# Building a relative-bias table on TensorE from masks made on GpSimd, in place of 305 VectorE steps

## The reference

```python
NUM_BUCKETS, MAX_DISTANCE = 32, 128
def t5_bucket(rel):
    n = jnp.maximum(rel, 0)
    max_exact = NUM_BUCKETS // 2
    log_ratio = jnp.log(jnp.maximum(n, 1).astype(jnp.float32) / max_exact) / math.log(MAX_DISTANCE / max_exact)
    large = max_exact + (log_ratio * (NUM_BUCKETS - max_exact)).astype(jnp.int32)
    large = jnp.minimum(large, NUM_BUCKETS - 1)
    return jnp.where(n < max_exact, n, large)
# in each block of 128 queries, for the selected keys:
bias = rel_bias[t5_bucket(q_pos[:, :, None] - k_pos)]          # rel_bias: 32 buckets x 8 heads
logits = jnp.einsum('bqhd,bqkhd->bqkh', q, k_sel) * a_scale + bias

def conformer_conv_mixer(h, w_in, conv_w, conv_b, ln_g, ln_b, w_out):
    val, glu_gate, z = jnp.split(h @ w_in, 3, axis=-1)
    u = causal_depthwise_conv(val * jax.nn.sigmoid(glu_gate), conv_w) + conv_b    # 31 taps, 2048 channels
    u = jax.nn.silu(layer_norm(u, ln_g, ln_b))
    return (u * jax.nn.silu(z)) @ w_out
```

## Time and profile before

| | us |
|---|---|
| median of three runs | 2084.09 |
| lowest, highest | 2082.16, 2085.47 |
| the profiled execution | 2082.0 |
| its span in the profile | 2080.2 |
| PE, DVE, ACT, POOL busy | 1895.7, 1620.2, 1079.7, 301.1 |
| mean granted PE clock | 0.962 |

### The profile page before, as it was taken

How to read it: one execution, slowest core, us unless ns; L and a number is a source line. 1 busy time by engine, 2 the same in 40 slices (tenths; PEclk the granted TensorE clock), 3 DMA queues, 4 the chain that set the end, 5 groups by cost and what they waited for, 6 DMA issues and landing times.

```text
span 2080.2 us, 32564 instructions
## 1 busy us (share of the span) xinstructions
PE 1895.7 (91%) x12370; PEld 1702.1 (82%) x12370; DVE 1620.2 (78%) x3041; ACT 1079.7 (52%) x1928; POOL 301.1 (14%) x380
## 2 busy tenths in 40 slices
PE   7897999989999999989979988988887987889997
PEld 6897888868889899889968876877886986779996
DVE  6988788978889998599976866778888576686666
ACT  6887644423354444478855444444445444454554
POOL 3876000000000000087800000020001000010000
PEclk9998999989999999999989999999999999999998
DMA  6344455634446776344535632537775352344652
GB/s 219 124 162 132 162 183 186 229 111 142 132 139 219 236 236 204 112 139 145 171 111 162 206 110 82 183 121 268 273 266 181 122 151 78 103 161 153 206 189 71
DMA packets 93756, 342.29 MB, mean 165 GB/s; under 512 B 10400, under 2 KB 10528, under 8 KB 92960
## 3 DMA queue, kind: packets, MB, share of 16 engines
q1 hardware_dynamic: 93600, 340.20, 49.9%
HBM read 339.11 MB, written 1.05 MB: 164 GB/s over the span
## 4 chain that ended last, share of the span: by engine, by line
PE 56%; DVE 30%; ACT 11%; issue 2%; DMA 0%; POOL 0%; SPq 0%; DVEq 0%; ACTq 0%
PE ps L98 55%; DVE wl L114 9%; ACT tmp L104 6%; DVE ps L124 5%; DVE tmp L124 3%; ACT wh L107 3%; DVE B L124 2%; DVE XS L114 2%; DVE tmp L114 1%; DVE B L114 1%; DVE tmp L119 1%; DVE raw L124 1%; ACT B L104 1%; DVE sm L136 1%; PE ps L101 1%
## 5 line engine op out<-in xcount | busy, mean ns | idle before, releaser
L98 PE MATMUL ps<-XS,wh 128*128 128x256 f32 (+1 forms) x5072 | 955.2, 290 | 39.9 <-DVE wl L114 27.4
L98 PEld LDWEIGHTS ps<-XS,wh 128*128 128x128 f32 (+1 forms) x5072 | 807.9, 195 | 65.4 <-issue 40.6
L114 DVE TENSOR_TENSOR wl<-raw,wh 128x1024 fp32r<-128x1024 f32 (+1 forms) x493 | 591.8, 1228 | 180.5 <-ACT wh L107 180.5
L98 PE MATMUL ps<-XS,wl 128*128 128x256 f32 (+1 forms) x2536 | 726.6, 287 | 0.0
L107 ACT CAST wh<-raw 128x1024 fp32r<-128x1024 f32 (+1 forms) x493 | 496.0, 1038 | 98.6 <-PE ps L98 92.8
L98 PEld LDWEIGHTS ps<-XS,wl 128*128 128x128 f32 (+1 forms) x2536 | 495.4, 195 | 0.0
L114 POOL TENSOR_TENSOR B<-B,tmp 128x236 f32<-128x236 f32 (+10 forms) x352 | 268.3, 800 | 775.1 <-ACT tmp L104 775.1
L98 PE MATMUL ps<-wh,os 128*128 128x512 f32 x864 | 291.0, 405 | 27.8 <-DVE os L114 18.9
L124 DVE SCALAR_TENSOR_TENSOR ps<-B,C,ps 128x254 f32<-128x254 f32 (+17 forms) x576 | 224.5, 469 | 8.3 <-ACT ps L104 8.3
L98 PEld LDWEIGHTS ps<-wh,os 128*128 128x128 f32 x864 | 167.9, 194 | 67.0 <-DVE os L114 20.8
L98 PE MATMUL ps<-wl,os 128*128 128x512 f32 x432 | 173.4, 401 | 0.0
(11 more groups left out here) (155 smaller groups left out, 1950.2 us busy)
## 6 DMA issues: line engine op xcount, KB each, us to landing
raw<-in_w SPq DMA_DIRECT2D x623, 512.0 KB, 4.4
raw<-in_w SPq DMA_DIRECT2D x12, 384.0 KB, 3.9
B<-in_ln SPq DMA_DIRECT2D x4, 1024.0 KB, 6.8
C<-in_cst SPq DMA_DIRECT2D x1, 1309.5 KB, 8.2
X<-in_x SPq DMA_DIRECT2D x2, 512.0 KB, 4.6
out_x<-X SPq DMA_DIRECT2D x4, 256.0 KB, 2.5
cb<-in_cb SPq DMA_DIRECT2D x1, 512.0 KB, 13.2
raw<-in_w SPq DMA_DIRECT2D x2, 256.0 KB, 3.3
```

Source lines behind the costliest of these rows:

```text
L98: return NOTHING if self.e is None else self.e.matmul(*a, **k)
L114: return NOTHING if self.e is None else self.e.tensor_tensor(o, a, b, op)
```

## The change

The table is computed as steps. A bias of bucket b is the sum over all buckets up to b of (bias of the bucket minus bias of the one before). For one key there are 32 comparisons "distance at least the start of bucket k", so four keys fill 128 rows of a mask. POOL makes such a mask (128 rows by 128 queries) with one `tensor_scalar` on the positions; PE multiplies it with a block-diagonal of the bias steps (128 x 32, `rblk`, four keys by eight heads) and gets the bias of 128 queries, four keys and eight heads. 96 masks make the table. Sixteen fill a PSUM bank, which ACT copies into `Bz` (`act_bias`). Masks lie in a ring of eight half buffers (`rep`).

The work stands in a0 and a1. POOL makes 16 masks at the start, then eight ahead of its additions for pair p (p = 0 to 3 in a0, 0 to 5 in a1). PE multiplies 16 ahead of everything, then eight at the end of iteration p (p = 1 to 4 in a0, 1 to 6 in a1). All calls of `bias` on DVE are gone. In stage c, the places that had no ada piece of layer 0 left now take 12 of layer 1, so that f0 has 28 in place of 40. The position row, now with 64 columns of key positions, and a first part of the constants are loaded ahead of X.

```diff
+NPOS = T + 64
+RING = 8
+BURSTS = (4, 6)
+
 CONSTS = (
-    [(f"a_norm{j}", 8) for j in range(2)]
+    [("bstart", 1), ("rblk", 32), ("rblk0", 32)]
+    + [(f"a_norm{j}", 8) for j in range(2)]
...
             if kind == "z" and i >= 2:
                 out.append((f"c.o{i - 1}", [("c_w_out", 0, 128 * (i - 1), 128, 0, D)], "split"))
             n_pair += 1
-            for _ in range(1):
-                a = next(u, None)
-                if a is not None:
-                    out.append(ada_piece(0, a))
+            a = next(u, None)
+            if a is not None:
+                out.append(ada_piece(0, a))
+            else:
+                out.append(ada_piece(1, next(u1)))
...
     b, u = plan_b()
-    out = plan_a(0) + b + plan_c(u) + plan_a(1)
-    u = iter(range(48))
+    u1 = iter(range(48))
+    out = plan_a(0) + b + plan_c(u, u1) + plan_a(1)
+    u = u1
     for l in range(2):
         out += plan_m(l, u) + plan_f(l, u)
...
         cst, posr, cbr, xin, out, lnr = self.ios
+        sp.dma_start(self.m["pos"][:], posr).then_inc(s["pos"].sem, 16)
+        sp.dma_start(self.m["C"][:, 0:NFIRST], cst[:, 0:NFIRST]).then_inc(s["const0"].sem, 16)
         for tb in range(2):
             sp.dma_start(self.X[:, tb, :], xin[:, tb, :]).then_inc(s[f"x{tb}"].sem, 16)
-        sp.dma_start(self.m["C"][:], cst).then_inc(s["const"].sem, 16)
-        sp.dma_start(self.m["pos"][:], posr).then_inc(s["pos"].sem, 16)
+        sp.dma_start(self.m["C"][:, NFIRST:NCONST], cst[:, NFIRST:NCONST]).then_inc(s["const"].sem, 16)
         for i in range(NRAW):
             self.load(sp, i)
         sp.dma_start(self.m["cb"][:], cbr).then_inc(s["cb"].sem, 16)
...
         if j == 0:
+            self.pe_bias(pe, 16, 7)
             pe.wait_ge(*s["const"][0])
         self.pe_entry(pe, A, self.xnt)
         bank, prior = self.a_order()
...
                 stats(2 * p - 3)
                 if p < 8:
                     pair("z", p - 2)
+            if 1 <= p <= BURSTS[j]:
+                self.pe_bias(pe, 8, 3)
         stats(14)
         stats(15)
         pe.wait_ge(*s["norm"][(A, "m"), "root"])
...
         if j == 0:
             self.act_rms(act, A, lambda tb, h: s[f"x{tb}"][0], "a_norm0", True)
+            self.act_bias(act, 0, 7)
             act.wait_ge(*s["cb"][0])
             act.wait_ge(*s["const"][0])
             act.activation(self.m["cb"][:], self.m["cb"][:], ACT.Silu).then_inc(s["lut"].up("silu"), 1)
...
         for p in range(9):
             at = 12 if p - 1 >= 2 else 0
+            if p % 2 and 3 <= p <= BURSTS[j] + 1:
+                self.act_bias(act, 2 * j + (p - 1) // 2, 3)
             if p < 8:
                 for n, (kind, m) in enumerate((("g", 0), ("g", 1), ("v", 0), ("v", 1))):
                     self.feed_act(act, f"{A}.{kind}{p}.{m}")
...
         n = 0
+        if j == 0:
+            self.pool_bias_begin(pool)
+            self.pool_masks(pool, 16)
+        else:
+            pool.wait_ge(*s["norm"][A, "root"])
         for p in range(8):
+            if p < BURSTS[j]:
+                self.pool_masks(pool, 8)
             before = {2 * p: None, 2 * p + 1: None}
...
-        return b[:, 0:3072].rearrange("p (h s) -> p h s", h=8), b[:, 3072:3456], b[:, 3456:3840]
-
-    def bias_step(self, dve, n):
...
-    def bias(self, dve, n):
+        return b[:, 0:3072].rearrange("p (h s) -> p h s", h=8), b[:, 3072:3072 + NPOS]
+
+    def mask(self, n):
+        i = n % RING
+        return self.m["rep"][i // 2][:, (i % 2) * 128:(i % 2) * 128 + 128]
+
+    def pool_bias_begin(self, pool):
+        s = self.s
+        Bz, pf = self.bias_views()
+        pool.wait_ge(*s["pos"][0])
+        pool.tensor_copy(pf, self.m["pos"][:]).then_inc(s["bias"].up("pf"), 1)
+        pool.wait_ge(*s["const0"][0])
+        pool.tt(self.c("rblk", 0, 32), self.c("rblk", 0, 32), self.c("rblk0", 0, 32), ALU.subtract).then_inc(
+            s["bias"].up("steps"), 1)
+        pool.wait_ge(*s["bias"]["pf"])
+
+    def pool_masks(self, pool, n):
+
+        s = self.s
+        Bz, pf = self.bias_views()
         for _ in range(n):
-            if self.nbias < 17 + 32 * 9:
-                self.bias_step(dve, self.nbias)
-                self.nbias += 1
+            x = self.nmask
+            self.nmask += 1
+            q, g = (0, x) if x < 32 else (128, x - 32)
+            if x >= RING:
+                pool.wait_ge(*s["table"][x - RING])
+            pool.ts(self.mask(x), pf[:, q:q + 128], pf[:, T + g:T + g + 1], self.c("bstart"), ALU.subtract,
+                    ALU.is_ge).then_inc(s["mask"].up(x), 1)
+
+    def pe_bias(self, pe, n, bank):
+
+        s = self.s
+        pe.wait_ge(*s["bias"]["steps"])
+        for _ in range(n):
+            x = self.nbias
+            self.nbias += 1
+            pe.wait_ge(*s["mask"][x])
+            if x and x % 16 == 0:
+                pe.wait_ge(*s["evac"]["bias", x // 16 - 1])
+            a = 32 * (x % 16)
+            pe.matmul(self.ps[bank][:, a:a + 32], self.mask(x), self.c("rblk", 0, 32), start=True, stop=True).then_inc(
+                s["table"].up(x), 1)
+
+    def act_bias(self, act, e, bank):
+        s = self.s
+        Bz, pf = self.bias_views()
+        k0 = 64 * e if e < 2 else 128 + 64 * (e - 2)
+        act.wait_ge(*s["table"][16 * e + 15])
+        act.activation(Bz[:, :, k0:k0 + 64], self.ps[bank].rearrange("p (k h) -> p h k", h=8), ACT.Identity).then_inc(
+            s["evac"].up(("bias", e)), 1)
 
 
 
...
                 if n >= 8:
-                    dve.wait_ge(*s["bias"]["add", 31, 7])
+                    dve.wait_ge(*s["evac"]["bias", 5])
...
         put(f"q_norm{l}", vec(inp["q_norm_g_2"][l]))
         put(f"kv_norm{l}", vec(inp["kv_norm_g_2"][l]))
-    put("rel_bias", np.broadcast_to(np.asarray(inp["rel_bias_2"]).reshape(1, 256), (128, 256)))
+    rel = np.asarray(inp["rel_bias_2"], np.float32)
+    steps = np.zeros((2, 4, 32, 4, 8), np.float32)
+    for k in range(4):
+        steps[0, k, :, k, :] = rel
+        steps[1, k, 1:, k, :] = rel[:-1]
+    put("rblk", steps[0].reshape(128, 32))
+    put("rblk0", steps[1].reshape(128, 32))
...
     pos = np.asarray(arrays["positions_2"], np.int32).reshape(T)
-    posr = np.empty((128, T + 2), np.int32)
+    posr = np.empty((128, NPOS), np.int32)
     posr[:, 0:T] = pos[None, :]
-    posr[:, T:T + 2] = pos.reshape(2, 128).T
```

More of the change, by code:

```diff
@@ L45 @@
 _at = 0
+NFIRST = 65
 for _name, _n in CONSTS:
@@ L151 @@
 SIGNALS = [
-    "const", "x0", "x1", "pos", "cb", "out",
+    "const", "const0", "x0", "x1", "pos", "cb", "out",
     "cast",
@@ L180 @@
     "bias",
+    "mask",
+    "table",
     "select",
@@ L240, in plan_b, with plan_c @@
     return out, u
-def plan_c(u):
+def plan_c(u, u1):
     out = []
@@ L373, in __init__ @@
         self.lows = self.casts = 0
-        self.nbias = 0
+        self.nbias = self.nmask = 0
         self.adas = {}
@@ L1071, in bias_views @@
         b = self.m["B"][2]
-        return b[:, 0:3072].rearrange("p (h s) -> p h s", h=8), b[:, 3072:3456], b[:, 3456:3840]
-    def bias_step(self, dve, n):
-        s, m = self.s, self.m
-        Bz, dist, bk = self.bias_views()
-        eq = [m["sc"][:], dist]
-        up = s["bias"]
-        if n == 0:
-            pf = self.tmp[5][:, 0:T + 2]
-            dve.tensor_copy(pf, m["pos"][:]).then_inc(up.up("pf"), 1)
-            dve.wait_ge(*up["pf"])
-            for o, k, w in ((0, 0, 128), (128, 1, 256)):
-                dve.ts(dist[:, o:o + w], pf[:, 0:w], pf[:, T + k:T + k + 1], -1.0, ALU.subtract,
-                       ALU.mult).then_inc(up.up(("n", k)), 1)
-            dve.wait_ge(*up["n", 1])
-            dve.ts(dist, dist, 0.0, None, ALU.max, None).then_inc(up.up("n"), 1)
-            dve.wait_ge(*up["n"])
-            dve.ts(bk, dist, 15.0, None, ALU.min, None).then_inc(up.up(("bk", 0)), 1)
-        elif n <= 16:
-            dve.wait_ge(*up["bk", n - 1])
-            dve.stt(bk, dist, float(bucket_starts()[n - 1]), bk, ALU.is_ge, ALU.add).then_inc(up.up(("bk", n)), 1)
-        else:
-            b, h = (n - 17) // 9, (n - 17) % 9 - 1
-            if h < 0:
-                dve.wait_ge(*up["bk", 16])
-                if b >= 2:
-                    dve.wait_ge(*up["add", b - 2, 7])
-                dve.ts(eq[b % 2], bk, float(b), None, ALU.is_equal, None).then_inc(up.up(("mask", b)), 1)
-            else:
-                r = self.c("rel_bias", b * 8 + h)
-                dve.wait_ge(*up["mask", b])
-                if b == 0:
-                    dve.ts(Bz[:, h, :], eq[0], r, None, ALU.mult, None).then_inc(up.up(("add", b, h)), 1)
-                else:
-                    dve.wait_ge(*up["add", b - 1, h])
-                    dve.stt(Bz[:, h, :], eq[b % 2], r, Bz[:, h, :], ALU.mult, ALU.add).then_inc(
-                        up.up(("add", b, h)), 1)
@@ L1364, in values @@
                 dve.tensor_copy(ct, self.ps[2][:, 0:32]).then_inc(s["soft"].up(("b", "ct")), 1)
-            self.bias(dve, 6)
         for n in range(3):
@@ L1372, in dve_b @@
```

(10 more changed lines are left out.)

5 lines of the change are left out of this document (3 added, 2 removed).

## The result

| | before | after |
|---|---|---|
| median, us | 2083.12 (2077.64 to 2085.47) | 2131.34 (2125.48 to 2135.06) |
| ratio | | 1.0233, 95% interval 1.0199 to 1.0266 |
| profiled execution | 2082.0 | 2125.48 |
| its span | 2080.2 | 2123.7 |

The forecast was 2087, with a range of 2070 to 2101: the sign was right, the size was not.

What follows compares the result with a forecast made beforehand. It took four engines in step to bound a0's convolution and DVE the first pairs of stage c. Terms +28 - 10.8 - 9.3 - 5 = +2.9 on the 2084.1 median gave 2087 us, range 2070 to 2101.

Steps and rivals of the forecast that it cites:

- I take 0.3, a burst of 2.4, between 1.9 and 3.4: Stage a: a POOL mask takes 0.3 us, so a burst of eight takes 2.4, ends 1.9 and 3.4.
- the large term: Stage a, added work: 11 us lost in a0 and 17 in a1, together 28, ends 17 and 38.
- A burst of 2.4 us would fit into POOL's idle 3.42 ahead of a pair.: Stage a: a mask burst fits POOL's idle time by length; only the order, waiting for PE, doesn't fit.
- There z ends 8 and then 11 us late: a1, pairs 4 and 5: fourth multiplications become 13.5 and 16.6 us late, plus 0.6 for a copy: 17 lost.
- The bytes ahead of the last constant stay nearly the same ... I take 0.: Start: DVE's first instruction stays near 9.9 us, 16 masks fit ahead; 0 change, ends 1 gained and 2 lost.
- Stage c: DVE loses 137 table steps and gains 12 adaptation pieces; PE's waits go: 10.8 us gained, ends 8 and 12.
- Stage b: Table steps leave places where PE was fed late: 5 us gained, ends 3 and 13.
- f0: Twelve adaptation pieces leave its last six half pairs, 8.44 us each in place of 10.03: 9.3 gained, ends 7 and 10.
- POOL's wait stays on POOL: Rival, stage a: ACT and PE have more room, only POOL's lack shows; loss 17 for 28, 2076 us; chance 0.26.
- The clock stays up in the attention's entry: Rival, 428.9 to 446 us: 2.4 GHz may hold with 0.55 us of wait left, 7 us back, 2080; chance 0.12.
- The clock falls in stage a: Rival: new waits of about 3 us for squares lower PE's clock, z slower, three times 3.3 us, 2097; chance 0.15.
- The transfers bound stage c: Rival: stage c's six buffers turn round too slowly for its pieces, half its gain goes, 2092 us; chance 0.10.

Runs made afterwards that it cites:

- short masks: Changed kernel with each POOL mask writing 32 of 128 columns with one operation, three quarters of the table left out: 2105.91 us, 1.0123.
- the kernel before with the wait: Kernel before, plus a POOL wait for PE's last z matmul of pair p-2 ahead of later pairs' additions in a0 and a1; no masks: 2097.97 us, 1.0086.
- masks of one operation: Changed kernel with masks made by one compare against a threshold added up once, in place of two operations: 2114.36 us, 1.0157.
- short masks and no held split: Changed kernel with masks of 32 columns and one operation, plus POOL waits for DVE's splits ahead of each convolution tap: 2097.88 us, 1.0079.
- the waits for DVE: Changed kernel plus a POOL wait ahead of each convolution tap for the DVE split in the same section of the pair: 2131.45 us, 1.0246.
- 16 buffers: Changed kernel with 16 mask buffers in place of 8: 2093.11 us, 1.0060; with POOL waits for DVE's splits added: 2084.37 us, 1.0010.

## Why the prediction was wrong, step by step

**The step that failed: "I take 0.3, a burst of 2.4, between 1.9 and 3.4".** A burst takes 6.23 us, outside the bounds, and by the short masks that makes 23 of the 46 us that the forecast missed. The bounds came from additions, which have two inputs and one operation; a mask has one input, two operations and pointers, and no row showed that. The nearest row was a different kind of instruction, so both ends were wrong together. The range of 2070 to 2101 was no help: the ends of the large term, 17 and 38, give 2076 and 2097, and the working doesn't say where the rest of it comes from.

**"A burst of 2.4 us would fit into POOL's idle 3.42 ahead of a pair."** With the price this fell as well. The burst ahead of pair 1, which waits for nothing, made POOL's additions of pair 1 5.5 us later in each block (7.2 us of masks less 1.7 of idle time).

**The loop.** The mechanism was right: POOL waits for the bias matmul, ACT for POOL. Its size was worked out pair by pair, and the later pairs came out too small. It is a closed loop: masks, additions, ACT's last multiplications and squares, PE's sums and z, PE's burst, and the next masks. Its length can be read off POOL's starts in a1, over three pairs each. Without masks or bursts (the kernel before with the wait):

```profile
923.99 5.16 POOL L114 TENSOR_TENSOR B<-B,tmp 128x236 f32<-128x236 f32 x8 [7.81 <-PE ps L98]
...
992.62 12.47 POOL L114 TENSOR_TENSOR B<-B,tmp 128x236 f32<-128x236 f32 x18 [4.84 <-PE ps L98]
```

With masks of 0.33 us:

```profile
926.62 2.68 POOL L125 TENSOR_SCALAR rep<-B 128x32 f32<-128x32 f32 x8 [9.94 <-PE ps L104]
...
1010.00 2.67 POOL L125 TENSOR_SCALAR rep<-B 128x32 f32<-128x32 f32 x8 [5.59 <-PE ps L104]
```

With masks of one operation:

```profile
931.78 4.66 POOL L125 TENSOR_SCALAR rep<-B 128x128 f32<-128x128 f32 x8 [7.96 <-PE ps L104]
...
1020.42 4.66 POOL L125 TENSOR_SCALAR rep<-B 128x128 f32<-128x128 f32 x8 [7.98 <-PE ps L104]
```

And the kernel after, whose 934.98 stands above:

```profile
1027.06 6.23 POOL L125 TENSOR_SCALAR rep<-B,C 128x128 f32<-128x128 f32 x8 [6.57 <-PE ps L104]
```

| kernel | masks of a burst | PE's burst | a pair, measured | 22.9 + masks + burst |
|---|---|---|---|---|
| wait alone | 0 | 0 | 22.9 | |
| short masks | 2.7 | 1.9 | 27.8 | 27.5 |
| one operation | 4.7 | 1.9 | 29.5 | 29.5 |
| after | 6.2 | 1.9 | 30.7 | 31.0 |

Masks and PE's burst add up nearly one for one: the last column is within 0.3 us of the measured one. The trace of the kernel with the wait alone is of its fastest execution (2091.3 us, median 2098.0), so 22.9 may be a little low. Against the 21.4 us of a pair before (POOL's starts of pairs 2 and 5 in a1, 918.07 and 982.41), a pair in the loop costs 9.3; four in a1 are 37, with the 5.5 of its first burst 43 of the 44 us. a0 has two, 18.6, with 5.5 and the start's 5.1: 29 of 30. The forecast's own prices put into this loop (2.4 + 1.9 + 22.9) give 5.8 a pair, 35 for six, where it had 28. In a0 the two agree (11.6 and 11); the difference lies in a1, in the step "There z ends 8 and then 11 us late", which adds 2 and 3 us for pairs 4 and 5 where the loop adds 5.8 each. With short masks and no held split, these two z ended 11.6 and 21.1 us late (against the entry of a1), with the masks of the change 21.5 and 32.6.

**"The bytes ahead of the last constant stay nearly the same ... I take 0."** The start cost 5.1. Sixteen masks, from 3.90 on, end at 16.7 us, not 8.7, PE's last bias matmul at 17.4, and its transposes begin there in place of 12.16. The constants came later too: DVE's first instruction, before at 9.87:

```profile
11.19 0.17 DVE L125 TENSOR_SCALAR sm<-sm 128x2 f32<-128x2 f32 x1 [11.19 <-DMA C<-in_cst]
```

**Held splits** were in no step. In the kernel after, taking them away gained nothing (the waits for DVE left it at 2131), which fits a DVE that is not on the loop's longest way: with those waits a pair took 31.2 us in a1, close to the 31.0 of the loop's sum. With short masks or 16 buffers they cost at least 9 to 10 us, since the waits on POOL cost something themselves. They would have been part of the answer had the price been right. Short masks without them are still 13 us above the forecast's sum, and 5 more were gained in b, c and f0 than it had. Of these 18 us, 7 are the loop's 5.8 a pair instead of its smaller steps, 2 the start (POOL's first addition at 34.9 in place of 33.0) and 2 the clock in m0 (below). POOL's starts put 5 more into the same six pairs, 40 us in sum where 5.8 a pair gives 35. The last 2 aren't settled.

**The gains.** Stage c: 10.8 forecast, 14.3 found, above the end of 12; what gave the last 2 us no run shows. Stage b: 5 forecast, 6.4 found. f0: 9.3 forecast, 9.8 found, within its ends. m0 was 2 us longer with the same instructions at a mean clock of 0.95 (1294 to 1402 us) in place of 1.00; some other kernels' profiles show the same and some don't, and why isn't known.

**The rivals.** "POOL's wait stays on POOL": no, ACT waited 12.25 us for DVE at 84.04 and PE 7.39 for the squares at 71.53. "The clock stays up in the attention's entry": no; the wait of 3.55 us ahead of it shrank to 0.96, and the granted clock was 0.59 in place of 0.50 over the stretch that answers to the one in the earlier trace rows. "The clock falls in stage a": it did, beside the step that failed. Behind the new waits of 4.13 and 4.06 us the z parts ran at 0.78 and 0.73 (the third row: one without a wait). The last row is the first of these z with the unit behind it; the same 115 matmuls are the row of the trace before:

```profile
94.25:101.70 7.45, 7.45 (x51) 7.45 (x51) 7.45 (x18) 7.42 (x15) 7.40 (x11) 0.78 0.48 141
134.30:142.15 7.85, 7.85 (x52) 7.85 (x52) 6.51 (x16) 4.33 (x11) 1.79 (x3) 0.73 0.22 68
156.60:164.10 7.50, 7.50 (x65) 7.50 (x65) 6.72 (x17) 4.59 (x14) 4.38 (x8) 1.00 0.36 127
94.25:111.72 17.47, 16.65 (x115) 16.57 (x115) 16.69 (x37) 10.96 (x25) 10.60 (x14) 0.81 0.40 121
```

```profile
79.90:93.54 13.64, 13.64 (x115) 13.61 (x114) 12.86 (x31) 10.69 (x24) 10.53 (x15) 1.00 0.52 194
```

Summed over such stretches of both blocks, PE is busy for 14 us more with the same matmuls than before, by an estimate from the two traces, and in the kernel with the wait alone for 5 or 6 more. z stands in the loop, so part of this is inside the 22.9 of the table above; how much of a turn the clock makes, no run separates.

"The transfers bound stage c": no; 258 GB/s and no idle time on PE.

## What to carry to other kernels

Price an instruction by a row of its own kind. If the trace has none, the bounds are wide, and a term that is multiplied by 80 deserves the widest. Where work is put on an idle engine, draw the whole loop: if the new work waits for something that waits for this engine, its duration adds to every turn, and idle time on the engine doesn't help; a deeper ring opens the loop (36 us here), and moving the work to places where both engines are idle anyway does better (2057 in place of 2131, with the same 96 masks and bias matmuls and the loads in their old order). A stall that stands out in the trace is not yet a cause: take it away first.
